# Block 2's last product, router, routing and first gather done by token halves; norm 2 by halves; one square root of block 1 moved

## The reference

```python
h = h + mixer_block(rmsnorm(h, norm1_g), ...)        # ends in merged @ w_o
u = rmsnorm(h, norm2_g)                              # 256 x 1024
grp_logits = u @ w_group                             # 8 groups
g = argmax(grp_logits); pg = softmax(grp_logits)[g]
sel = (u @ w_router).reshape(T, 8, 8)[:, g]          # the 8 experts of that group
top_v, top_i = top_k(sel, 2)                         # 2 of 64 experts for each token
weights = pg * softmax(top_v)
for e in range(64):                                  # over the tokens of expert e
    y = (silu(x @ w1[e]) * (x @ w3[e])) @ w2[e]      # 3 x 2 MB of weights each
    out[tokens of e] += weight * y
h = h + out
```

## Time and profile before

| | us |
|---|---|
| median of 3 runs | 1685.43 (1682.55 to 1689.26) |
| the profiled execution's own time | 1688.89 |
| its span in the trace | 1687.1 |
| PE busy | 1276.8 (76%) |
| DVE busy | 338.3 (20%) |
| ACT busy | 189.6 (11%) |
| POOL busy | 13.0 (1%) |
| moved by DMA | 502.26 MB, 298 GB/s over the span |

### The profile page before, as it was taken

How to read it: one execution, slowest core, us unless ns; L and a number is a source line. 1 busy time by engine, 2 the same in 40 slices (tenths; PEclk the granted TensorE clock), 3 DMA queues, 4 the chain that set the end, 5 groups by cost and what they waited for, 6 DMA issues and landing times.

```text
span 1687.1 us, 15862 instructions
## 1 busy us (share of the span) xinstructions
PE 1276.8 (76%) x6695; PEld 730.5 (43%) x6695; DVE 338.3 (20%) x846; ACT 189.6 (11%) x393; POOL 13.0 (1%) x25
## 2 busy tenths in 40 slices
PE   7998999999899999987665647556574756656465
PEld 4665677775477888653221212222121222212121
DVE  3344233333154200031010110101011110101101
ACT  2324212211112100010000000000000000000000
POOL 3000000000000000000000000000000000000000
PEclk9999999999998999979787878878787787878778
DMA  9430244444432344927999999999999999999996
GB/s 302 164 136 1 87 156 158 154 159 159 155 142 100 112 155 158 386 87 328 427 428 428 428 428 428 428 428 427 428 428 428 427 428 428 427 428 428 428 427 254
DMA packets 89870, 502.26 MB, mean 298 GB/s; under 512 B 6694, under 2 KB 34578, under 8 KB 65233
## 3 DMA queue, kind: packets, MB, share of 16 engines
q1 hardware_dynamic: 88960, 500.00, 73.2%
q0 software_dynamic: 848, 1.36, 0.4%
HBM read 500.29 MB, written 1.05 MB: 297 GB/s over the span
## 4 chain that ended last, share of the span: by engine, by line
PE 58%; DMA 37%; DVE 2%; issue 1%; ACT 1%; SPq 1%; DVEq 0%; ACTq 0%
DMA expert_ring<-in_w 25%; PE ps L1089 17%; PE ps L613 13%; DMA dense_ring<-in_w 12%; PE ps L936 9%; PE ps L608 7%; PE ps L954 5%; PE ps L792 2%; DMA dense_ring<-in_w_in 1%; PE ps L1079 1%; PE ps L984 0%; PE ps L718 0%; PE ps L706 0%; PE ps L1005 0%; PE ps L689 0%
## 5 line engine op out<-in xcount | busy, mean ns | idle before, releaser
L1089 PE MATMUL ps<-expert_ring,hT 128*32 128x512 f32 x592 | 147.0, 733 | 123.3 <-DMA expert_ring<-in_w 69.4
L1089 PE MATMUL ps<-expert_ring 128*32 128x512 f32 x608 | 143.7, 723 | 100.5 <-DMA dense_ring<-in_w 54.1
L1089 PE MATMUL ps<-dense_ring,hT 128*32 128x512 f32 x432 | 146.9, 746 | 57.1 <-DMA expert_ring<-in_w 57.1
L1089 PE MATMUL ps<-dense_ring,expert_ring 128*32 128x512 f32 x416 | 143.6, 727 | 56.3 <-DMA expert_ring<-in_w 56.3
L613 PE MATMUL ps<-hT,dense_ring 128*128 128x256 f32 x768 | 172.3, 384 | 0.1
L613 PEld LDWEIGHTS ps<-hT,dense_ring 128*128 128x128 f32 x768 | 147.8, 193 | 22.7 <-issue 1.6
L936 PE MATMUL ps<-hT,dense_ring 128*128 128x256 f32 x704 | 155.5, 382 | 1.2 <-ACT hT L1831 1.2
L936 PEld LDWEIGHTS ps<-hT,dense_ring 128*128 128x128 f32 x704 | 135.0, 192 | 24.0 <-issue 5.8
L1779 DVE TENSOR_TENSOR moe_hid<-moe_hid,ps 64x512 f32<-64x512 f32 x32 | 22.1, 690 | 588.6 <-ACT moe_hid L2060 588.6
L1089 PEld LDWEIGHTS ps<-expert_ring,hT 128*32 128x32 f32 x592 | 37.8, 132 | 194.5 <-issue 194.5
L1089 PEld LDWEIGHTS ps<-expert_ring 128*32 128x32 f32 x608 | 37.4, 130 | 170.2 <-issue 170.2
(11 more groups left out here) (346 smaller groups left out, 1065.1 us busy)
## 6 DMA issues: line engine op xcount, KB each, us to landing
expert_ring<-in_w SPq DMA_DIRECT2D x108, 2048.0 KB, 29.6
dense_ring<-in_w SPq DMA_DIRECT2D x84, 2048.0 KB, 29.0
dense_ring<-in_w_in SPq DMA_DIRECT2D x18, 2048.0 KB, 8.2
dense_ring<-in_w_up SPq DMA_DIRECT2D x22, 1024.0 KB, 8.5
dense_ring<-in_w_down SPq DMA_DIRECT2D x11, 1024.0 KB, 4.9
dense_ring<-in_w_out SPq DMA_DIRECT2D x2, 2048.0 KB, 14.4
dense_ring<-in_w_conv_out SPq DMA_DIRECT2D x2, 2048.0 KB, 7.8
dense_ring<-in_w_attn_out SPq DMA_DIRECT2D x2, 2048.0 KB, 7.7
```

The costliest lines, as they stand in the source:

```text
L1089: last = mm(ps[k * CAP:(k + 1) * CAP, UP, :], x[:, c, (k % 2) * CAP:(k % 2 + 1) * CAP], (w1, w3)[k // 2][k % 2][:, c * DE:(c + 1) * DE], s ...
```

## The change

1. The expert end: `w_o` is done by token halves (both units for tokens 0 to 127, then both for the others). PE turns the un-normed `h` (`turn_h`) and multiplies it with router weights that already hold the norm's gain (a DVE product in the convolution stage); DVE scales the logits by the row's 1/rms. The router weights are therefore laid out as (c p) instead of (p c). Logits, routing, ranks, `choose` and the gather run for each half; the normed rows `uN` for the gather come from ACT, without gain, and the gain is put on when the gathered slices are taken from PSUM (two instructions for each slice instead of one). The four matmuls that put `h` into the sums and the register read of the fullest expert stand behind the first pair's first product, or behind the selection.
2. Norms: the squares of a half come in two pieces of 512 columns, and ACT adds and roots without DVE in between. Norm 2 runs by halves: the last feed-forward product completes half 0 first, and the second half's transposes stand behind the first four chunks of `q0`.
3. The loads of the router weights and of two gains, and the 512 KB of the broadcast norm gain, leave the start: the first ones are issued after block 1's output product, the last is now two small loads.
4. Block 1's square root stands before the bank copy.

PE's order from `w_o` to the first expert product. Before: L608 is the product, L570 the transposes of norm 3, L1054 the logits, L1060 puts `h` into the sums, L1065 to L1069 are the ranks, L1079 the gather, L1089 the experts.

The diff's core:

```diff
+            pool.wait_ge(bank_emptied_dve, emptied("D", PROD["wout_h1"], 1))
+            for dst, n in ((q_gain2, "q_norm_g_2"), (k_gain2, "k_norm_g_2")):
+                pool.dma_start(dst, t[n].rearrange("a b -> (a b)").partition_broadcast(P)).then_inc(late_in, 16)
+            pool.dma_start(router_w[:, :, 0:NG], t["w_group_2"].rearrange("(c p) n -> p c n", p=P)).then_inc(late_in, 16)
+            pool.dma_start(router_w[:, :, NG:], t["w_router_2"].rearrange("(c p) n -> p c n", p=P)).then_inc(late_in, 16)
...
+                if final:
+                    pe.wait_ge(ff_act, 2 * k + 3)
+                    pe.wait_ge(ff_down, k + 1)
+                    pe.sem_inc(dense_used, 1)
+                    for half in range(2):
+                        for n in range(2):
+                            for a in range(2):
+                                last = mm(ps[:, 4 + half * 2 + n, :], act_T[:, s, a, half * P:(half + 1) * P],
+                                          dn[:, a, n * 512:(n + 1) * 512], start=(a == 0), stop=(a == 1))
+                        last.then_inc(ff_down, 1)
+                    return
...
-            pe.wait_ge(ff_down, FCH // 2 + 1)
+            norm_turn(2, xn2, 0)
+            pe.wait_ge(ff_down, FCH // 2 + 2)
...
+                        if a == "q0" and q % 2 == 0:
+                            wait_hT(12 + 2 * q)
                         part(a, hT, True, q)
+                        if a == "q0" and q == 0:
+                            norm_turn(2, xn2, 1)
...
+            def wo(half, n):
+                u, step = UNIT[f"wo{n}"], PROD[f"wo_h{half}"]
+                if not half:
+                    pe.wait_ge(dense_loaded[u % RING], dense_value(u))
+                wait_bank(step, n)
+                for c in range(KC):
+                    last = mm(ps[:, BANKS[step][n], :], mrg[:, c, half * P:(half + 1) * P], slot_view(u)[:, c, :],
+                              start=(c == 0), stop=(c == KC - 1))
+                last.then_inc(bank_filled, 1)
+            def turn_h(half, n, banks):
+                pe.wait_ge(bank_emptied_dve, emptied("D", PROD[f"wo_h{half}"], n))
+                for c in range(4):
+                    last = turn(ps[:, banks[c // 2], c * P:(c + 1) * P], h[:, half, (4 * n + c) * P:(4 * n + c + 1) * P], ident)
+                last.then_inc(h_turned, 1)
+            def logits(half, n):
+                if n:
+                    pe.wait_ge(hT_dve, 17 + half)
+                if n == half:
+                    pe.wait_ge(hT_act, 17 + 2 * half)
+                else:
+                    pe.wait_ge(hT_act, 17 + half)
+                for c in range(4 * n, 4 * n + 4):
+                    last = mm(ps[:, 6 - half, 0:NG + NE], hT[:, c, half * P:(half + 1) * P], router_w[:, c, :],
+                              start=(c == 0), stop=(c == KC - 1))
+                if n:
+                    last.then_inc(logits_ready, 1)
+            before, ones = const("before"), const("ones")
+            pe.wait_ge(merged, 4)
+            wo(0, 0)
             release_last()
+            wo(0, 1)
+            turn_h(0, 0, (4, 4))
+            wo(1, 0)
+            turn_h(0, 1, (5, 5))
+            logits(0, 0)
+            logits(0, 1)
+            turn_h(1, 0, (7, 7))
+            wo(1, 1)
+            for n in range(2):
+                pe.wait_ge(bank_filled, filled(PROD["wo_h1"], n))
+                pe.sem_inc(dense_used, 1)
+            logits(1, 0)
+            turn_h(1, 1, (4, 3))
             pe.wait_ge(assigned, 1)
+            mm(ps[:, 6, 0:NE], before, assign[:, 0, :], start=True, stop=True).then_inc(ranks_ready, 1)
+            logits(1, 1)
             uview = uN.rearrange("p a (n c) -> p a c n", c=KC)
...
             pe.wait_ge(sel_ready, 1)
+            pe.wait_ge(u_ready, 1)
             for s in range(4):
-                if s >= 2:
-                    pe.wait_ge(xg_ready, s - 1)
-                gather_slice(s, (GT, DN)[s % 2])
+                gather_first(s, 0)
+            mm(ps[:, 7, 0:NE], ones, assign[:, 0, :], start=True, stop=False)
+            pe.wait_ge(assigned, 2)
+            mm(ps[:, 7, 0:NE], before, assign[:, 1, :], start=False, stop=True).then_inc(ranks_ready, 1)
+            mm(ps[:, 6, NE:2 * NE], ones, assign[:, 0, :], start=True, stop=False)
+            mm(ps[:, 6, NE:2 * NE], ones, assign[:, 1, :], start=False, stop=True).then_inc(ranks_ready, 1)
+            pe.wait_ge(sel_ready, 2)
+            pe.wait_ge(u_ready, 2)
+            for s in range(4):
+                gather_first(s, 1)
...
-                if p:
+                if p == 0:
+                    for half in range(2):
+                        for n in range(2):
+                            mm(ps[:, 2 * half + n, :], ident, h[:, half, n * 512:(n + 1) * 512], start=True, stop=False,
+                               skip_group_check=True)
+                    pe.wait_ge(slots_ready, 1)
+                else:
...
-            dve.wait_ge(ff_down, LAST + 1)
             for half in range(2):
+                dve.wait_ge(ff_down, LAST + 1 + half)
                 for n in range(2):
                     o = h[:, half, n * 512:(n + 1) * 512]
-                    last = v.tensor_tensor(o, o, ps[:, 4 + half * 2 + n, :], ALU.add)
-                last.then_inc(h_ready, 1)
-            dve.wait_ge(h_ready, 4)
-            for half in range(2):
+                    v.tensor_tensor(o, o, ps[:, 4 + half * 2 + n, :], ALU.add).then_inc(h_ready, 1)
+                dve.wait_ge(h_ready, 2 * half + 2)
                 norm_rows(2, xn2, half)
-            norm_take(2)
+                norm_take(2, half)
...
+            def add_last(half, n):
+                b = filled_bank(f"wo_h{half}", n)
+                o = h[:, half, n * 512:(n + 1) * 512]
+                v.tensor_tensor(o, o, b, ALU.add).then_inc(bank_emptied_dve, 1)
+            def take_h(half, bank, n):
+                dve.wait_ge(h_turned, 2 * half + 2)
+                v.tensor_copy(hT[:, 4:4 + n, half * P:(half + 1) * P],
+                              ps[:, bank, 0:n * P].rearrange("p (c s) -> p c s", c=n)).then_inc(hT_dve, 1)
+            def route_half(half):
+                dve.wait_ge(rstd_ready, 7 + half)
+                dve.wait_ge(logits_ready, half + 1)
+                l, e = lg[:, half, :], elm[:, half, :]
+                then(v.tensor_scalar(l, ps[:, 6 - half, 0:NG + NE], rstd[:, half:half + 1], None, ALU.mult))
+                then(v.max(g8[:, half, :], l[:, 0:NG]))
+                then(v.max_index(gi8u[:, half, :], g8[:, half, :], l[:, 0:NG]))
+                then(v.tensor_copy(gi8[:, half, :], gi8u[:, half, :]))
+                then(v.tensor_scalar(gohb[:, half, :], const("iota64")[:, 0:NG], gi8[:, half, 0:1], NEG, ALU.not_equal, ALU.mult))
+                then(v.tensor_tensor(e.rearrange("p (a b) -> p a b", a=NG), l[:, NG:].rearrange("p (a b) -> p a b", a=NG),
+                                     gohb[:, half, :].unsqueeze(2).to_broadcast([P, NG, EPG]), ALU.add))
+                then(v.max(e8[:, half, :], e))
+                then(v.max_index(ei8u[:, half, :], e8[:, half, :], e))
+                then(v.tensor_copy(ei8[:, half, :], ei8u[:, half, :]))
+                v.tensor_scalar(oh1[:, half, :], const("iota64"), ei8[:, half, 0:1], None, ALU.is_equal)
+                then(v.tensor_scalar(oh2[:, half, :], const("iota64"), ei8[:, half, 1:2], None, ALU.is_equal))
+                v.tensor_tensor(assign[:, half, :], oh1[:, half, :], oh2[:, half, :], ALU.add).then_inc(assigned, 1)
+            def slots_half(half):
...
+            add_last(0, 0)
+            add_last(0, 1)
+            norm_rows(3, None, 0)
+            add_last(1, 0)
+            take_h(0, 5, 4)
+            route_half(0)
+            add_last(1, 1)
+            take_h(1, 4, 2)
+            slots_half(0)
+            choose(slice(0, OCT), OCT, sel_ready, (0,))
+            norm_rows(3, None, 1)
+            route_half(1)
+            v.tensor_scalar(ngm, g8[:, :, 0:1], -1.0, None, ALU.mult)
...
+            slots_half(1)
+            choose(slice(0, OCT), OCT, sel_ready, (1,))
+            dve.wait_ge(ranks_ready, 3)
...
+            def squares(half, n, junk):
+                then(a_(junk[:, half, n * 512:(n + 1) * 512], h[:, half, n * 512:(n + 1) * 512], ACT.Square,
+                        accum_out=ssq[:, half, n:n + 1]))
+                col = slice(half, half + 1)
+                if n == 0:
+                    then(a_(msq[:, col], ssq[:, half, 0:1], ACT.Identity, scale=1.0 / D, bias=eps))
+                else:
+                    a_(rms[:, col], ssq[:, half, 1:2], ACT.Sqrt, scale=1.0 / D, bias=msq[:, col]).then_inc(rms_ready, 1)
...
             exp_step(4)
+            act.wait_ge(heads_ms, NORMED["gla"])
+            a_(ogla_ss, ogla_r, ACT.Sqrt).then_inc(heads_rms, 1)
             b = filled_bank("gout", 1)
             a_(sil[:, 2:4, :].rearrange("p a b -> p (a b)"), b, ACT.Copy).then_inc(bank_emptied_act, 1)
```

(19 more changed lines are left out.)

348 lines of the change are left out of this document (151 added, 197 removed), and 2 rows, old and new, of the table PRODUCTS.

## The result

The changed kernel took 1656.05 us (median of 4 runs, 1649.25 to 1657.97) against 1685.36 us of the kernel before in the same comparison (4 runs, 1682.55 to 1689.26). The ratio is 0.9817, 95% interval 0.9802 to 0.9832: 1.8% faster. Forecast were 1654.6, and 1649 to 1665 as the range. The profiled execution took 1657.97, its span is 1656.1 against 1687.1: 31.0 us less, where the sum had said 30.8. How these 31.0 are made up is the subject of what follows, since two of the parts are not as forecast.

A forecast was written before the change was run, and what follows sets the result against it. The end was taken as the first pair's first product plus a fixed-length DMA stream; gains 2.8 + 4.0 + 0.7 + 5.3 + 18.0 = 30.8 us gave 1654.6, range 1649 to 1665 (8 in 10).

The forecast's parts named there:

- start: Start of the kernel: PE's wait for a weight unit goes, product starts at 23.7; gain 2.8 us, bounds 0 and 3.5.
- square root: Block 1: the root moved earlier removes most of PE's wait for DVE; gain 4.0 us, bounds 1.5 and 4.3.
- norm 1: Norm 1: last half's squares shorter, a memset and DVE's step go; 0.7 us, up to 3 if the clock stays up.
- norm 2: Norm 2 by halves, with `q0` passes ahead of half 1's transposes: gain 5.3 us, bounds 3 and 6.5.
- end stage: From `merged` to the first expert product: 68.0 us becomes 50.0; gain 18.0, bounds 13 and 19.
- stream: Expert weights behind the first product: fixed length, 183 units or 898 us at 427 GB/s, following that product one for one.
- the gather's pass: End stage: about 0.216 us a pass, half of `w_o`'s pass for half the columns; 16 passes take 3.5.
- One half's routing: End stage, DVE: 3.0 us for one half where both took 4.8; bounds 2.4 and 4.8.
- A lower clock after each shorter wait: Rival, PE's several waits of 1 to 2 us: clock comes back lower, gain 22.9, time 1662.5; chance 0.13.
- the stream doesn't follow: Rival, expert weights: units 7 and 8 or the w2 units hold it, only 12.8 arrive, 1672.6; chance 0.03.
- PE stays slow through the cut-up stage: Rival, end stage: lower clock throughout makes it 95 us instead of 50, time 1699; chance 0.02.
- SP holds the start: Rival, start: SP's 3 us issues hold the DMA, not traffic; 1657.4, within the forecast's own range; no separate chance given.

The follow-up runs named there:

- root_back: Changed kernel with block 1's square root put back behind the bank copy and the copy of turned probabilities: 1659.86 us, ratio 0.985.
- ahead16: Changed kernel plus sixteen unused 512-column passes between the two halves' gathers, ahead of the first pair's first product: 1660.87 us, ratio 0.9856.
- behind16: Changed kernel plus sixteen unused 512-column passes just behind the first pair's first product: 1655.64 us, ratio 0.9826.
- loads_back: Changed kernel with the first norm's squares in one 1024-column piece and the four late loads (two gains, router weights) back at the start: 1653.75 us, ratio 0.9831.
- fill_narrow: Changed kernel, first norm in one piece, unused matmuls in PE's waits (start, norm 1, attention, last pair) and between the 32 passes of 15 columns: 1647.79 us, ratio 0.9779.
- fill_end: As fill_narrow, with 5 instead of 2 unused matmuls behind the last pair's third weight unit: 1648.58 us, ratio 0.979.

## Why the prediction was right, point by point

Its working from the table, before minus after, in us:

| term | forecast (bounds) | measured | how |
|---|---|---|---|
| start | 2.8 (0 to 3.5) | -0.7 | 128.11 to 128.83, last 256-column product of block 1 |
| square root, norm 1 | 4.0 + 0.7 | 5.3 | from there to B: 60.79 to 55.51 |
| norm 2 | 5.3 (3 to 6.5) | 6.3 | L962 to C: 60.30 to 54.03 |
| rest of B to C | 0 | -0.4 | 5.88 less 6.27 |
| attention | 0 | 3.0 | C to D |
| end stage | 18.0 (13 to 19) | 17.05 | D to E |
| stream | 0 | 0.5 | E to end |
| sum | 30.8 | 31.0 | |

- **The end stage** went by the layout: w_o's half 0 14.0 (13.9 forecast), fourth bank from 24.2 to 31.1 (24.5 to 31.4), last logits from 33.3 to 34.4 (33.6 to 34.6), routing of half 1 3.0 (3.0), second gather from 39.65 (39.4). What was mis-sized is the gather's pass: 16 took 4.15 and 4.21 instead of 3.5. PE's timeline, weight loads first:

```profile
720.16 3.91 PEld L1129 LDWEIGHTS ps<-gains,expert_ring 128*128 128x128 f32 x16
720.22 4.15 PE L1129 MATMUL ps<-gains,expert_ring 128*128 128x256 f32 x16
```

The sixteen weight loads alone take 3.91: 0.24 each, more than the 0.216 forecast for a pass. That each pass has weights of its own is not enough to explain it. The products of `part` (L615) have that too, with the same 128x128 weights and 256 columns, and their 768 passes take 171.1, which is 0.22 each. The loads differ (busy us, mean ns of one):

```profile
L615 PEld LDWEIGHTS ps<-hT,dense_ring 128*128 128x128 f32 x768 | 146.8, 192 | 22.3 <-issue 1.8 <-DVE expert_ring L1661 0.5
L1129 PEld LDWEIGHTS ps<-gains,expert_ring 128*128 128x128 f32 x32 | 7.8, 336 | 0.5 <-DVE gains L1783 0.5
```

The gather reads its weights from `uN` at a distance of eight elements and `part` reads neighbours, but no run changed that, so the cause stays open. The pass had been taken as half of `w_o`'s; the five in a microsecond of the earlier trace rows, cut ones at both ends among them, fit 0.24 as well as 0.216. The row to read was the gather's own load.

- **One half's routing** cost 3.0 us where both had cost 4.8 in one: the Trainium skill (VectorE: DVE Perf Modes, section on the TRN2 errata) has a fixed extra latency in every instruction of DVE and ACT that reads SBUF, and the trace agrees in kind, 3.0 + 3.0 against 4.8. It does not hurt, since half 0's lies under `w_o`'s last bank.

- **The square root.** DVE's product ended at 135.05 and PE turned at 135.32 without waiting. The load of the table and the root behind it:

```profile
132.06 1.28 ACT L2024 ACT_TABLE_LOAD   x1
133.35 0.21 ACT L2024 ACTIVATE expert_ring<-expert_ring 128x8 f32<-128x8 f32 x1
```

1.29 us from load to root, as in the earlier trace rows. By the 2.66 us that the Trainium skill gives (ScalarE: Activation LUTs, What ACT_TABLE_LOAD costs) root and transposes would have come 1.4 later; no drain shows behind the load here, and the measurement decides. The term was 4.0 with 4.3 as its upper bound, and root_back puts it at 4.5 to 4.7.

- **Norm 2** brought 6.3; 6.1 was the figure for no fall of the clock behind the transposes, and that is the case that came. The 5.3 was a mean of two cases, and a single run shows only one of them.

- **The start** is the step that failed. The wait on the DMA went as said, even by 3.1 us and not 2 (21.5 against 24.6). But "the product starts at 23.7" needed `cmp_in` at the full clock; it ran partly at 1.2 GHz, the product started at 25.53, and a longer stay at the low clock near 104 took another 1.6. In the second profile of the same kernel the start is 23.59, the 16 passes run at full clock, and all 2.8 are there. The case was named (0, if "the lower clock merely moves elsewhere"), and it came out still lower.

- **The attention's 3.0 us** are the clock's; the instructions there are the same. The chain of the kernel before, then of after, behind waits of PE that are the same in both, 1.83 and 0.78 us:

```profile
507.25 2.07 PE ps L984 x4
509.32 5.54 PE ps L613 x16
```

```profile
496.81 1.13 PE ps L994 x4
497.94 3.45 PE ps L615 x16
```

Behind these waits the clock fell in the kernel before and not in after. Only one profile of the kernel before is kept, and one of the ten profiles of changed kernels without fillers has a fall there, so whether it was chance, or the kernel before falls there more often, stays open. No text of the prediction had this; what it gave and what the start lost cancel, so that the sum came out closer than its parts.

- **Rivals.** A lower clock after each shorter wait (22.9) came true at some waits only, and not in the end stage. That the stream doesn't follow is excluded by ahead16 and behind16; that PE stays slow through the cut-up stage, by a clock of 1.00 in it; that SP holds the start, by the landing of `kv_tok`'s unit.

Left open is what decides, at a wait of two or three microseconds, whether the clock falls. Filled waits had no fall, unfilled ones had it mostly but not always, the same wait of 2.92 us in two of three profiles. The Trainium skill (TensorE: Matmul & The Clock Gate, The HAM clock gate) says that the monitor runs free of the kernel, so that the phase at which work meets it differs by run. The two profiles of the same kernel agree with that; no run here shows the monitor itself. Nor is it known why the fall near 400 to 410 us came in ten profiles and not in ahead16, loads_back, fill_narrow and fill_end, whose instructions there are the same.

## What to carry to other kernels

Where a long stream starts with one event, count only what stands ahead of that event: work moved behind it is free as far as the stream covers it, and every microsecond ahead of it is paid in full. Split the chain behind the last product, not necessarily the product: here the order of `w_o` was worth 0.8 of 17 us. And before a term of 2 us is believed, take two profiles of the same kernel and cut both at the same instructions. Unused work in PE's waits, with the first norm in one piece, made this kernel some 6 us faster and its times more comparable: they spread over 0.65 to 3.7 us with the waits ahead of D filled, and over 3.4 to 11 without.

## What was not expected of the hardware

- PE's clock can fall without a gap in its work: behind 32 passes of 15 columns, 1.96 us in all, in 8 of the 12 profiles that have them bare, at a cost of 1.6 to 3.2 us each. The eight passes behind them (L750) use 64 rows as they do, and which of them matter is not shown. With four wide passes between them it did not fall in two of two, which is too few to call it shown.
- The clock column read 1.00 in the first 24 us while passes of 256 columns took 764 ns instead of 379; sixteen transposes there took 3.91 us when PE had done nothing before and 1.95 after five unused matmuls.
- 416 KB of small loads moved the landing of a 2 MB unit by 2.9 us (14.3 us from issue at 9.53 with them, 11.2 from 9.71 without), three times what 427 GB/s would ask. With the 512 KB gain as well, in the kernel before, it is 14.6: the larger load adds only 0.3.
- Loads of 128 x 128 weights don't all take the same time: 336 ns in the gather, whose passes of 256 columns stand 0.24 us apart, and 192 ns in `part`, whose passes of 256 columns stand 0.22 apart.
